# Down units of the expert layer stored with two 128-column blocks interleaved, and x's halves moved in SBUF

## The chip, the cores and the metric

The kernel runs on one core of a Trainium2 chip. The metric is the device time of one execution in microseconds (us). Engines are named as in the profile: PE is TensorE (its weight loads are listed apart, as PEld), DVE is VectorE, ACT is ScalarE, POOL is GpSimd, SP is the engine whose queue issues most DMAs.

## The reference

A transformer block pair in float32 on 256 tokens of width 1024. The part that the change is in is the expert layer (`peer_ffn`): of 16384 experts every token and head picks 16, and the layer needs, for each picked expert e, `gelu(u_e . x)` and then a weighted sum of rows `v_e`:

```python
u = expert_down[eidx]
a = jax.nn.gelu(jnp.einsum('thkd,td->thk', u, xb), approximate=False)
coef = (g * a.astype(jnp.float32)).astype(xb.dtype)
return jnp.einsum('thk,thkd->td', coef, expert_up[eidx])
```

The kernel doesn't gather. It computes `u_e . x` for all 16384 experts and all 256 tokens (the first pass over the experts, with `expert_down`), makes a dense matrix of coefficients that is zero where an expert is not picked, and multiplies it by all of `expert_up` (the second pass).

## The kernel before

**Precision.** Large products are made in fp32r, a float32 format that PE streams at one column a cycle. Each operand is split in a high half (a rounded copy, by ACT) and a low half (the rest, by DVE), and a product is three matmuls: high by high, high by low, low by high.

**Units.** The experts come from HBM in 256 units of 128 partitions x 1024 words (512 KB), units 0 to 127 for the first pass and 128 to 255 for the second. SP loads a unit to `raw_u` (4 buffers), ACT writes `hi_u` (3 buffers, L1586), DVE writes `lo_u` (2 buffers, L2299). A unit of the first pass holds 128 experts; its partition p and block k of 128 words hold element 128k+p of each expert's row, so that block k is the stationary operand of one step over the width.

**The first pass.** `down_unit(u, out)` waits for the unit's halves and runs over k = 0..7. In each step it issues three matmuls with 256 moving columns: stationary `hi_u` block k with moving `xh[:, k, :]` (L938), the same stationary block with moving `xl[:, k, :]` (L941), stationary `lo_u` block k with moving `xh[:, k, :]` (L942). These are 24 matmuls a unit and 3072 in all. Each has its own weight load of 128 columns, 128 consecutive words of each partition. The program prints the operands of a matmul as moving, stationary: `bank<-xh,hi_u` streams `xh` over weights from `hi_u`.

**What DVE does beside it.** In the first two thirds of the pass DVE also picks the experts (steps of `route`, listed at L2196, L2203, L2210, L2213, L2217, L2239 and others). A hand-written table (`ROUTE`) places these steps between the `lo_u` writes of units 0 to 81, in program order. `lo_u` of unit u can be written when the first matmul of unit u-1 has been done (its buffer is then free, `unit_used`), and PE starts unit u when `lo_u` of u is there (`unit_split`). From pair 20 on, PE also runs groups of four 128-column float32 matmuls of one-hot rows (L950, `oh`) between units.

**Addresses.** Tensors are placed by word offset in the partition. All base addresses that matter here are told modulo 128 words, since each block k starts a multiple of 128 words after its tensor's start. `hi_u` and `lo_u` (and `whi`, `wlo`, the same place) start at 80. Before the change `xh` and `xl` both start at 64, which is 16 words below the weights. `xmh` and `xml`, which share the space, start at 96. In the two stages that multiply by the up-projections of the later feed-forward layers (22 slots of 48 matmuls each; they run through 1200 to 1290 us and 1510 to 1590 us) the moving halves `nh`, `nl` both start 16 words below the weights too. `xh` and `xl` are also operands of 456 matmuls of the first projections (L605 to L607, from 11.8 to 78 us), where the weights `whi`, `wlo` are packed.

Of the kernel before, what the change touches and what calls it, by code (L numbers as in the profile page):

```python
# [36 lines left out]
P = 128  # L37
# [3 lines left out]
KD = D // P  # L41
# [10 lines left out]
UNIT = KD * P  # L52
# [145 lines left out]
def program(nc, t):  # L198
    with ExitStack() as ctx:
# [32 lines left out]
        keep = Area(0)  # L232
        h = keep("h", TB, D)

        CROSSING_AT = keep.at
        keep.at += 64
        XH = keep.at
        xh = keep("xh", KD, T, dt=F32R)
        xl = keep("xl", KD, T, dt=F32R)
        keep.at += 64  # L240
        mixed = Area(XH + 32)
        xmh = mixed("xmh", KD, T, dt=F32R)
        xml = mixed("xml", KD, T, dt=F32R)
        cols = keep("cols", N_COLS)
# [310 lines left out]
        def _(pe):  # L555
# [121 lines left out]
            for tb in range(TB):  # L677
                pe.wait_ge(S(f"x_loaded{tb}"), 16)
                for k in range(KD):
                    i, c = k // 2, k % 2  # L680
                    mm = pe.transpose(banks[i][:, c * T + tb * P:c * T + (tb + 1) * P], h[:, tb, k * P:(k + 1) * P], ident)
# [4 lines left out]
            for i in range(4):  # L686

                if i < 3:
                    pe.wait_ge(S("first_low"), i + 1)
                    w = [x.rearrange("p (k n) -> p k n", k=KD) for x in (whi[:, 0, :], wlo[:, 0, :])]  # L690
                else:
                    w = slot("in", 0)
                mm = rows_of(0, i, bank, outs_T(bank), w, xn)
# [4 lines left out]
            for half in range(2):  # L698
                if half == 0:
                    pe.wait_ge(S("second_low"), 1)  # L700
                    w = [x.rearrange("p (k n) -> p k n", k=KD) for x in (whi[:, 1, :], wlo[:, 1, :])]
                else:
                    w = slot("in", 1)
                for c in range(2):
                    for k in range(4 * half, 4 * half + 4):
                        mm = three(bank[:, c * T:(c + 1) * T], [p[:, k, c * P:(c + 1) * P] for p in w], [x[:, k, :] for x in xn],
                                   k == 0 and c == 0, k == KD - 1, True)
            close(mm)
            free_slot()
            w = slot("in", 2)  # L710
# [4 lines left out]
            mm = product_T(bank[:, T:2 * T], w, P, xn)  # L715
# [5 lines left out]
            w = slot("in", 5)  # L721
# [28 lines left out]
            for tb in range(TB):  # L750
                mm = pe.transpose(bank[:, tb * P:(tb + 1) * P], avT[:, tb * P:(tb + 1) * P], ident)
# [3 lines left out]
            for q in range(2):  # L755
                for tb in range(TB):
                    mm = pe.transpose(bank[:, 8 * q + 4 * tb:8 * q + 4 * tb + 4],
                                      gates[0:4, 5 + q, tb * P:(tb + 1) * P], ident[0:4, 0:4])
            close(mm)
            pe.wait_ge(S("const_loaded"), 16)  # L760
            for g in range(2):
                bank = open_("mrow", g)
                for c in range(2):
                    hd = 2 * g + c
                    mm = pe.matmul(bank[:, c * T:(c + 1) * T], cst("sel")[0:4, hd * P:(hd + 1) * P], gates[0:4, 7, :],
                                   start=True, stop=True)
# [7 lines left out]
            for hd in range(4):  # L774
                bank = open_("mscore", hd)
                o = HALF * (hd % 2)
                q, k = qkT[o:o + HALF, hd // 2, :], qkT[o:o + HALF, 2 + hd // 2, :]
# [11 lines left out]
            for hd in range(4):  # L789
                bank = open_("mout", hd)  # L790
                for tb in range(TB):
                    out = bank[:, tb * (P + 1):(tb + 1) * (P + 1)]
                    mm = pe.matmul(out, mE[:, hd, tb * P:(tb + 1) * P], mv[:, 0, hd, :], start=True, stop=(tb == 0))
                    if tb == 1:
                        mm = pe.matmul(out, mE[:, hd, T:T + P], mv[:, 1, hd, :], start=False, stop=True)
# [4 lines left out]
            for hd in range(8):  # L800
                bank = open_("wT", hd)
                pe.transpose(bank[:, 0:P], wS[:, hd * P:(hd + 1) * P], ident)
                for kb in range(2):
                    a = 1024 + hd * T + kb * P
                    mm = pe.transpose(bank[:, P * (1 + kb):P * (2 + kb)], wS[:, a:a + P], ident)
# [5 lines left out]
            for g in range(2):  # L811
                bank = open_("wout", g)
                for c in range(2):
                    for kv in range(2):
                        hd = 4 * kv + 2 * g + c
                        o = HALF * kv
                        out = bank[o:o + HALF, c * T:(c + 1) * T]
                        pe.matmul(out, av[:, 0, o:o + HALF], wT[:, hd, 0:T], start=True, stop=False)
                        mm = pe.matmul(out[:, P:T], av[:, 1, o:o + HALF], wT[:, hd, T:T + P], start=False, stop=True)
# [4 lines left out]
            for tb in range(TB):  # L824
                bank = open_("hmT", tb)
                for c in range(4):
                    mm = pe.transpose(bank[:, c * P:(c + 1) * P], hm[:, tb, c * P:(c + 1) * P], ident)
# [39 lines left out]
            for g in range(2):  # L867
                drained("xq", 2 * g, 2 * g + 1)
                for tb in range(TB):
                    bank = open_("xscore", 2 * g + tb)  # L870
                    for c in range(2):
                        hd = 2 * g + c
                        for dc in range(2):
                            mm = pe.matmul(bank[:, c * T:(c + 1) * T], xqT[:, 2 * hd + dc, tb * P:(tb + 1) * P],
                                           kxT[:, 2 * hd + dc, :], start=(dc == 0), stop=(dc == 1))
# [44 lines left out]
            def unit(u):  # L920

                pe.wait_ge(S("unit_split"), u + 1)
                return hi_u[:, u % HIGH_U, :], low_unit(u)
# [6 lines left out]
                    freeing(ins)  # L930

            def down_unit(u, out):
                w = unit(u)
                for k in range(KD):
                    if u == 0 and k % 2 == 0:
                        pe.wait_ge(S("xn_split"), k // 2 + 1)
                    kp = slice(k * P, (k + 1) * P)
                    mm = pe.matmul(out, w[0][:, kp], xh[:, k, :], start=(k == 0), stop=False)  # L938
                    if k == 0:
                        unit_done(mm, u)  # L940
                    pe.matmul(out, w[0][:, kp], xl[:, k, :], start=False, stop=False)  # L941
                    mm = pe.matmul(out, w[1][:, kp], xh[:, k, :], start=False, stop=(k == KD - 1))  # L942
                return mm

            def spread_group(g):
# [47 lines left out]
            for c in range(P - 2):  # L993
                if c % 2 == 0:
                    pe.wait_ge(S("coef_low"), c // 2 + 1)
                w = unit(P + c)
# [1696 lines left out]
def pack(inp):  # L2693

    g = {k: np.asarray(v) for k, v in inp.items()}
    one = lambda k: g[k].reshape(g[k].shape[1:]) if g[k].shape[0] == 1 else g[k]

    def slots(w):

        out = []  # L2700
        for a in range(0, w.shape[1], 256):
            piece = w[:, a:a + 256]
            piece = np.pad(piece, ((0, 0), (0, 256 - piece.shape[1])))
            out.append(piece.reshape(KD, P, 256).transpose(1, 0, 2).reshape(P, -1))
        return out

    def down(w):

        return [w[i:i + 256].reshape(2, P, D).transpose(1, 0, 2).reshape(P, -1) for i in range(0, w.shape[0], 256)]

    def up(w):

        f = w.shape[1] // 2
        return slots(np.concatenate([np.concatenate([w[:, a:a + P], w[:, f + a:f + a + P]], 1) for a in range(0, f, P)], 1))

    w_in = one("w_in")
    zeros = lambda n: np.zeros((D, n), np.float32)

    order = np.concatenate([np.arange(hd * HALF, (hd + 1) * HALF) for c in range(4) for hd in (c, c + 4)])

    gates = [w_in[:, 1536:1540], zeros(28), w_in[:, 1540:1544], zeros(P - 36)]
    w_in = np.concatenate([w_in[:, 0:512]] + gates + [w_in[:, 2056:2184], w_in[:, 1544:2056][:, order],
                           w_in[:, 2184:2312], zeros(P), w_in[:, 512:1536]], 1)
    w_out = one("w_out")
    w_out = np.concatenate([w_out[0:512], w_out[512:][order]], 0)
    w_odd = g["odd_w_in_2"][0]
    w_xv = slots(one("w_xv"))

    w_even = g["even_w_in_2"][0]
    w_even = np.concatenate([w_even[:, 0:1024], w_even[:, 1536:3584], w_even[:, 1024:1536]], 1)  # L2730
    ws = (slots(w_in) + slots(one("w_xk")) + w_xv[0:1] + slots(w_out) + w_xv[1:2] + slots(one("w_xq")) + w_xv[2:4]
          + slots(one("w_xo")) + slots(one("w_pq")) + slots(w_even) + slots(g["even_w_out_2"][0])
          + up(g["ffn_w_up_2"][0]) + down(g["ffn_w_down_2"][0]) + slots(w_odd[:, :256]) + slots(w_odd[:, 3072:]) + slots(w_odd[:, 256:3072])
          + slots(g["odd_w_out_2"][0]) + up(g["ffn_w_up_2"][1]) + down(g["ffn_w_down_2"][1]))
    assert len(ws) == N_SLOTS
    cols = np.zeros((P, N_COLS), np.float32)

    def put(name, a):
        cols[:a.shape[0], COLS[name][0]:COLS[name][0] + COLS[name][1]] = a

    chan = lambda a: a.reshape(-1, P).T
    for name, a in [("g_mix", g["g_mix"][0]), ("g_cross", g["g_cross"][0]), ("g_mem", g["g_mem"][0]),
                    ("g_ffn", g["g_ffn"][0]), ("mix0", g["mix_norm_g_2"][0]), ("mix1", g["mix_norm_g_2"][1]),
                    ("ffn0", g["ffn_norm_g_2"][0]), ("g_final", g["g_final"]), ("ffn1", g["ffn_norm_g_2"][1]), ("conv_b", g["conv_b"][0]),
                    ("cb0", g["ffn_conv_b_2"][0]), ("cb1", g["ffn_conv_b_2"][1])]:
        put(name, chan(a))
    for name, a in [("conv_w", g["conv_w"][0]), ("cw0", g["ffn_conv_w_2"][0]), ("cw1", g["ffn_conv_w_2"][1])]:
        put(name, a.reshape(a.shape[0], -1, P).transpose(2, 1, 0).reshape(P, -1))
    put("b_i", g["b_igate"].reshape(4, 1))
    put("b_f", g["b_fgate"].reshape(4, 1))  # L2750
    put("sb_q", np.tile(g["sb_q_gain_2"][0], 2)[:, None])
    put("sb_k", np.tile(g["sb_k_gain_2"][0], 2)[:, None])
    rows = np.concatenate([g["g_mhead"][0], g["sinks"][0], g["ret_out_gain_2"][0], g["gla_out_gain_2"][0], g["g_final"]])
    down_units = g["expert_down"][0].reshape(P, P, KD, P).transpose(0, 3, 2, 1).reshape(P, P, UNIT)
    experts = np.concatenate([down_units, g["expert_up"][0].reshape(P, P, UNIT)], 0)
    return {
        "x": g["x"][0], "mem": g["mem"][0], "weights": np.stack(ws), "cols": cols, "rows": rows,
        "const": constants(),
        "keysT": np.stack([g["sub_keys1"][0].T, g["sub_keys2"][0].T], 1),
        "experts": experts,  # L2760
        "walpha": np.concatenate([g["gla_w_alpha_2"][0], g["gla_b_alpha_2"]], 0),
    }
# [20 lines left out]
```

## Time and profile before

| | |
|---|---|
| median of 3 runs | 1668.85 us (1668.18, 1668.85, 1672.76) |
| profiled execution, first to last instruction | 1670.5 us; its page gives no other time |
| PE busy | 1652.9 us (99%), 12006 matmuls |
| DVE busy | 1237.3 us (74%) |
| ACT busy | 935.2 us (56%) |
| POOL busy | 242.8 us (15%) |
| first pass over the experts | 268.9 to 690.9 us |

Matmuls are pipelined: a listed duration (279 ns) overlaps the next matmul, so PE is "busy" 99% whatever its pace. What a matmul costs is the distance from its start to the next one's start, called its cadence below.

### The profile page before, as it was taken

Reading aid. Unit: us, or ns where it says so; the run is one execution under the profiler, and the core shown is the slowest. Engines: PE = TensorE matmul, PEld = TensorE weight load, DVE = VectorE, ACT = ScalarE, POOL = GpSimd, SP = SyncE. Lnnn points to the kernel's source line nnn. Section 1 sums busy time; section 2 is a strip of 40 time slices with the busy share of each in tenths; the row PEclk is TensorE's granted clock in tenths of the full one; section 3 lists DMA queues with packets and bytes.
Section 4 is the critical chain, followed back from the end, with each engine's and each line's share of the span. In section 5 each row is a group of like instructions: output and inputs, shape, how many; then the busy total and the mean of one; then the engine's idle time right before and its main releaser. Section 6 shows DMA issues by size and latency. Waiting matters only on the chain.

```text
span 1670.5 us, 30280 instructions
## 1 busy us (share of the span) xinstructions
PE 1652.9 (99%) x12006; PEld 1542.5 (92%) x12006; DVE 1237.3 (74%) x1896; ACT 935.2 (56%) x1139; POOL 242.8 (15%) x333
## 2 busy tenths in 40 slices
PE   8999999999999999999999999999999999999999
PEld 8999999999999999988888888999999888899987
DVE  6875467999998666667676676887888565769974
ACT  7885565555546555545555454786545357565542
POOL 0000000004667676211010110000000000100000
PEclk9999999999999999999999999999999999999999
DMA  7445344776555555777777776533555544345553
GB/s 304 152 152 180 120 159 157 231 233 213 189 178 191 190 189 191 270 240 238 245 235 239 241 238 222 221 133 139 184 185 195 180 174 152 124 156 203 200 188 115
DMA packets 73804, 323.40 MB, mean 194 GB/s; under 512 B 8663, under 2 KB 9047, under 8 KB 55744
## 3 DMA queue, kind: packets, MB, share of 16 engines
q1 hardware_dynamic: 58736, 285.18, 50.1%
q0 software_dynamic: 5568, 19.38, 3.7%
q10 hardware_dynamic: 9360, 16.92, 2.7%
q8 instruction: 95, 1.56, 0.4%
q14 instruction: 45, 0.37, 0.1%
HBM read 303.62 MB, written 17.83 MB: 192 GB/s over the span
## 4 chain that ended last, share of the span: by engine, by line
PE 83%; DVE 12%; ACT 4%; issue 1%; DMA 0%; SPq 0%; ACTq 0%; DVEq 0%
PE bank L605 14%; PE bank L606 13%; PE bank L607 13%; PE bank L986 7%; PE bank L985 7%; PE bank L987 7%; PE bank L938 5%; PE bank L942 5%; PE bank L941 5%; DVE lo_u L2299 3%; PE bank L950 2%; DVE wlo L1914 2%; DVE oh L2310 1%; ACT whi L1350 1%; DVE pos L2196 1%
## 5 line engine op out<-in xcount | busy, mean ns | idle before, releaser
L1586 ACT ACTIVATE hi_u<-raw_u 128x1024 fp32r<-128x1024 f32 x256 | 271.8, 1062 | 279.6 <-PE bank L985 165.2
L1914 DVE TENSOR_TENSOR wlo<-raw,whi 128x2048 fp32r<-128x2048 f32 (+1 forms) x141 | 314.7, 2232 | 105.6 <-PE bank L605 83.3
L1350 ACT ACTIVATE whi<-raw 128x2048 fp32r<-128x2048 f32 x137 | 263.1, 1920 | 77.6 <-PE bank L605 74.7
L938 PE MATMUL bank<-xh,hi_u 128*128 128x256 f32 x1024 | 291.9, 285 | 1.5 <-DVE lo_u L2299 1.2
L2299 DVE TENSOR_TENSOR lo_u<-raw_u,hi_u 128x1024 fp32r<-128x1024 f32 x192 | 237.9, 1239 | 70.4 <-PE bank L938 62.4
L941 PE MATMUL bank<-xl,hi_u 128*128 128x256 f32 x1024 | 285.4, 279 | 0.0
L942 PE MATMUL bank<-xh,lo_u 128*128 128x256 f32 x1024 | 285.3, 279 | 0.0
L605 PE MATMUL bank<-nh,whi 128*128 128x256 f32 x904 | 253.4, 280 | 0.5 <-DVE wlo L1914 0.4
L607 PE MATMUL bank<-nh,wlo 128*128 128x256 f32 x904 | 251.9, 279 | 0.0
L606 PE MATMUL bank<-nl,whi 128*128 128x256 f32 x904 | 251.9, 279 | 0.0
L519 POOL TENSOR_SCALAR oh<-kept,sel_T 128x128 f32<-128x128 f32 x256 | 199.9, 797 | 249.3 <-ACT sel_T L1636 166.4
L985 PE MATMUL bank<-hi_u,chi 128*128 128x512 f32 x512 | 200.9, 392 | 0.3 <-DVE lo_up L2299 0.3
L987 PE MATMUL bank<-hi_u,clo 128*128 128x512 f32 x512 | 198.7, 388 | 0.0
L938 PEld LDWEIGHTS bank<-xh,hi_u 128*128 128x128 f32 x1024 | 193.0, 188 | 3.4 <-issue 1.5
L941 PEld LDWEIGHTS bank<-xl,hi_u 128*128 128x128 f32 x1024 | 193.4, 189 | 0.0
L942 PEld LDWEIGHTS bank<-xh,lo_u 128*128 128x128 f32 x1024 | 192.8, 188 | 0.0
L607 PEld LDWEIGHTS bank<-nh,wlo 128*128 128x128 f32 x904 | 171.3, 190 | 0.0
L605 PEld LDWEIGHTS bank<-nh,whi 128*128 128x128 f32 x904 | 169.8, 188 | 1.5 <-DVE wlo L1914 1.1
L606 PEld LDWEIGHTS bank<-nl,whi 128*128 128x128 f32 x904 | 170.0, 188 | 0.0
L2299 DVE TENSOR_TENSOR lo_up<-raw_u,hi_u 128x1024 fp32r<-128x1024 f32 x64 | 78.4, 1226 | 96.1 <-PE bank L985 96.1
L985 PEld LDWEIGHTS bank<-hi_u,chi 128*128 128x128 f32 x512 | 96.1, 188 | 23.0 <-DVE lo_up L2299 0.7
L605 PE MATMUL bank<-whi,nh 128*128 128x256 f32 x408 | 115.4, 283 | 0.8 <-DVE nl L1895 0.7
(417 smaller groups left out, 3358.7 us busy)
## 6 DMA issues: line engine op xcount, KB each, us to landing
raw<-in_weights SPq DMA_DIRECT2D x138, 1024.0 KB, 4.8
raw_u<-in_experts SPq DMA_DIRECT2D x256, 512.0 KB, 4.2
aside<-a_out ACTq DMA_DIRECT2D x64, 256.0 KB, 3.6
a_in<-aside POOLq DMA_DIRECT2D x64, 256.0 KB, 3.7
const<-in_const SPq DMA_DIRECT2D x1, 1409.0 KB, 9.0
const<-in_const POOLq DMA_DIRECT2D x1, 1409.0 KB, 6.4
h<-in_x SPq DMA_DIRECT2D x2, 512.0 KB, 5.1
raw<-in_weights SPq DMA_DIRECT2D x2, 512.0 KB, 7.6
```

Source lines behind the costliest of these rows:

```text
L605: freeing(pe.matmul(out, lhs[0], rhs[0], start=first, stop=False, skip_group_check=skip))
L606: pe.matmul(out, lhs[0], rhs[1], start=False, stop=False, skip_group_check=skip)
L607: return pe.matmul(out, lhs[1], rhs[0], start=False, stop=last, skip_group_check=skip)
L938: mm = pe.matmul(out, w[0][:, kp], xh[:, k, :], start=(k == 0), stop=False)
L941: pe.matmul(out, w[0][:, kp], xl[:, k, :], start=False, stop=False)
L942: mm = pe.matmul(out, w[1][:, kp], xh[:, k, :], start=False, stop=(k == KD - 1))
L985: first = pe.matmul(out, c_hi, w[0][:, cs], start=(c == 0), stop=False)
L987: mm = pe.matmul(out, c_lo, w[0][:, cs], start=False, stop=(c == P - 1))
L1350: a(A(whi[:, n % HIGH, :], raw[:, n % RAW, :], ACT.Copy), S("weights_hi"))
L1586: a(A(hi_u[:, u % HIGH_U, :], raw_u[:, u % RAW_U, :], ACT.Copy), S("unit_high"))
L1914: v(V.tensor_tensor(wlo[:, n % LOW, place], raw[:, n % RAW, place], whi[:, n % HIGH, place].bitcast(F32), ALU.subtract), S("weights_split" ...
L2299: v(V.tensor_tensor(low_unit(u), raw_u[:, u % RAW_U, :], hi_u[:, u % HIGH_U, :].bitcast(F32), ALU.subtract), S("unit_split"))
```

## The change

The host stores the blocks of a down unit in pairs, with the words of blocks 2j and 2j+1 alternating; the elementwise splits by ACT and DVE and the DMAs run over the same 1024 words as before. A weight load of block k now reads every second word of 256 consecutive ones, starting at word k % 2. Besides, `xh` moves to 16 (modulo 128 words, 64 below the weights, counted round) and `xl` to 112 (32 above them). The total space and the places of `xmh`, `xml`, `chi`, `clo` and everything else stay. No engine's instructions change in number or order, and no wait is added or removed.

```diff
         CROSSING_AT = keep.at
-        keep.at += 64
+        keep.at += 16
         XH = keep.at
         xh = keep("xh", KD, T, dt=F32R)
+        keep.at += 96
         xl = keep("xl", KD, T, dt=F32R)
-        keep.at += 64
-        mixed = Area(XH + 32)
+        keep.at += 16
+        mixed = Area(CROSSING_AT + 96)
...
             def down_unit(u, out):
-                w = unit(u)
+                w = [x.rearrange("p (k n c) -> p k c n", c=2, n=P) for x in unit(u)]
...
-                    kp = slice(k * P, (k + 1) * P)
-                    mm = pe.matmul(out, w[0][:, kp], xh[:, k, :], start=(k == 0), stop=False)
+                    mm = pe.matmul(out, w[0][:, k // 2, k % 2, :], xh[:, k, :], start=(k == 0), stop=False)
                     if k == 0:
                         unit_done(mm, u)
-                    pe.matmul(out, w[0][:, kp], xl[:, k, :], start=False, stop=False)
-                    mm = pe.matmul(out, w[1][:, kp], xh[:, k, :], start=False, stop=(k == KD - 1))
+                    pe.matmul(out, w[0][:, k // 2, k % 2, :], xl[:, k, :], start=False, stop=False)
+                    mm = pe.matmul(out, w[1][:, k // 2, k % 2, :], xh[:, k, :], start=False, stop=(k == KD - 1))
...
-    down_units = g["expert_down"][0].reshape(P, P, KD, P).transpose(0, 3, 2, 1).reshape(P, P, UNIT)
+    down_units = g["expert_down"][0].reshape(P, P, KD // 2, 2, P).transpose(0, 4, 2, 1, 3).reshape(P, P, UNIT)
```

## Rows read from the trace of the kernel before

**Rows 1.** The page: span, and busy time, share and instructions of each engine.
```profile
span 1670.5 us, 30280 instructions
PE 1652.9 (99%) x12006; PEld 1542.5 (92%) x12006; DVE 1237.3 (74%) x1896; ACT 935.2 (56%) x1139; POOL 242.8 (15%) x333
```

**Rows 2.** Stretches of the first pass: busy (instructions) of PE, PEld, DVE, ACT, POOL; clock.
```profile
268.89:525.03 256.14, 254.69 (x2181) 252.70 (x2180) 243.11 (x610) 139.33 (x163) 92.79 (x118) 1.00 0.63 205
525.03:690.88 165.85, 165.85 (x1445) 165.85 (x1444) 104.93 (x198) 90.14 (x114) 109.32 (x143) 1.00 0.58 198
```

**Rows 3.** The same stretches, L950's one-hot matmuls alone.
```profile
268.89:525.03 256.14, 29.47 (x224) 1.00 0.63 205
525.03:690.88 165.85, 37.95 (x288) 1.00 0.58 198
```

**Rows 4.** Timeline of PE: first matmuls of units 16 and 17, 24 matmuls apart.
```profile
318.08 0.28 PE L938 MATMUL bank<-xh,hi_u 128*128 128x256 f32 x1
...
320.90 0.28 PE L938 MATMUL bank<-xh,hi_u 128*128 128x256 f32 x1
```

**Rows 5.** Timeline of PE: first matmuls of units 33 and 34, 24 matmuls apart.
```profile
366.39 0.28 PE L938 MATMUL bank<-xh,hi_u 128*128 128x256 f32 x1
...
369.12 0.28 PE L938 MATMUL bank<-xh,hi_u 128*128 128x256 f32 x1
```

**Rows 6.** Timeline of PE: runs of plain float32 matmuls, start and length of each run.
```profile
168.53 7.07 PE L874 MATMUL bank<-kxT,xqT 128*128 128x256 f32 x32
1362.62 1.03 PE L592 MATMUL bank<-kept,h 128*128 128x128 f32 x8
271.72 3.73 PE L907 MATMUL bank<-keysT,pqT 128*128 128x128 f32 x32
```

**Rows 7.** Timeline of PE: the second pass, 512 moving columns.
```profile
800.02 0.39 PE L985 MATMUL bank<-hi_u,chi 128*128 128x512 f32 x1
800.25 0.39 PE L986 MATMUL bank<-lo_up,chi 128*128 128x512 f32 x1
800.48 0.39 PE L987 MATMUL bank<-hi_u,clo 128*128 128x512 f32 x1
800.71 0.39 PE L985 MATMUL bank<-hi_u,chi 128*128 128x512 f32 x1
```

**Rows 8.** Stretches of two later stages, PE alone: busy (matmuls), clock.
```profile
1200.00:1290.00 90.00, 90.00 (x767) 1.00 0.53 188
1510.00:1590.00 80.00, 80.00 (x709) 1.00 0.55 195
```

**Rows 9.** Waits of DVE from 268 to 525 us: total, times, longest.
```profile
DVE lo_u L2299 <- PE bank L938: 4.0, 6, 2.1
```

**Rows 10.** Waits of DVE from 525 to 691 us.
```profile
DVE lo_u L2299 <- PE bank L938: 58.4, 45, 2.5
```

**Rows 11.** Timeline of DVE in the first stretch, with no wait in it.
```profile
434.23 1.29 DVE L2213 TENSOR_TENSOR onehot<-posf,kept 128x1024 f32<-128x1024 f32 x1
435.55 1.28 DVE L2299 TENSOR_TENSOR lo_u<-raw_u,hi_u 128x1024 fp32r<-128x1024 f32 x1
436.87 1.27 DVE L2217 TENSOR_TENSOR onehot<-onehot,i16f 128x1024 f32<-128x1024 f32 x1
438.17 1.28 DVE L2299 TENSOR_TENSOR lo_u<-raw_u,hi_u 128x1024 fp32r<-128x1024 f32 x1
```

**Rows 12.** Timeline of DVE in the second stretch; in brackets the idle time ahead.
```profile
603.13 1.28 DVE L2299 TENSOR_TENSOR lo_u<-raw_u,hi_u 128x1024 fp32r<-128x1024 f32 x1 [1.24 <-PE bank L938]
604.45 1.17 DVE L2310 TENSOR_SCALAR oh<-kept,sel_T 128x128 f32<-128x128 f32 x4
606.76 1.28 DVE L2299 TENSOR_TENSOR lo_u<-raw_u,hi_u 128x1024 fp32r<-128x1024 f32 x1 [1.14 <-PE bank L938]
```

**Rows 13.** Matmuls with `xh` outside the first pass: count, durations, first and last start.
```profile
L605 PE MATMUL bank<-xh,whi x88: 276/281/582, 11.8 to 44.6; 128*128 128x256 f32 x88
L605 PE MATMUL bank<-whi,xh x64: 276/279/388, 49.0 to 77.5; 128*128 128x256 f32 x64
```

## The prediction

> **What bounds the kernel now.** I read the page first: PE is busy 1652.9 of 1670.5 us [rows 1]. That number says only that PE's queue is rarely empty, because listed durations overlap. So I read the starts. In the first pass the timeline shows two paces for the same instructions. Unit 16 takes 320.90 - 318.08 = 2.82 us for 24 matmuls, 117.7 ns each [rows 4]. Unit 33 takes 2.73 us, 113.6 ns each [rows 5]. The granted clock is 1.00 in both, the 2.4 GHz level, at which 256 columns take 106.7 ns; so 7 ns or 11 ns a matmul are lost. The same pair of paces stands in two later stages that run the same form of matmul: 90.00 us over 767 records, less the about three that began earlier, is 117.8 ns, and 80.00 over 706 is 113.3 ns [rows 8]. Both numbers are multiples of one step over 106.7: three matmuls take 320 ns of streaming, and 340 or 353.3 ns here, which is 3 or 5 steps of 6.67 ns (16 cycles). In the second pass three matmuls of 512 columns take 800.71 - 800.02 = 0.69 us against 0.64 of streaming, about 7 steps [rows 7].
>
> Plain float32 runs lose less. 32 matmuls of 256 columns take (7.07 - 0.38)/31 = 216 ns, two cycles a column being 213.3. Eight transposes take (1.03 - 0.27)/7 = 109 ns for 128 columns (106.7 of streaming), and the key products (3.73 - 0.27)/31 = 111.6 ns [rows 6]. What differs is the reading speed. In those runs a column of the moving operand takes two cycles. In fp32r it takes one, while the weights of the next matmul, 128 words, must come in during about the same 113 ns. So the stream walks through SBUF at about twice the pace of the load beside it, and the distance between the two changes by 128 words in each matmul. In the plain runs of 128 columns both walk 128 words in the same time.
>
> Next, who sets the time of the pass. It has two parts. From 268.89 to 525.03 us (units 0 to 79) DVE is busy 243.1 of 256.1 us and waits for PE only 4.0 us [rows 2, 9]; its timeline is back to back, `lo_u` between steps of the routing [rows 11]. There DVE sets the time, or nearly. From 525.03 to 690.88 us (units 80 to 127) DVE waits for PE 58.4 us, over a microsecond ahead of each `lo_u` [rows 10, 12], and PE sets the time.
>
> **The change, part by part.** The instructions of all engines, their order and waits stay, and so do the bytes and shapes of the DMAs and splits; these cost 0. What changes is only how PE's two readings run.
>
> *The load with a step of two words.* It now walks 256 words while the stream walks 256. If the lost steps come from the two meeting in SBUF at equal addresses modulo some period, a distance that stays constant (64 or 32 words, never 0) has no meeting. The trace of before shows no load with a step, so I bound the new cadence. Below: 109 ns, the transposes. Above, if the load reads twice the stretch and pays twice, 2 x 106.7 = 213 ns. Between them the marks are 111.6 (key products), 113.3, 117.8 and one step more on each matmul, 124.4. I take 110: the plain runs, whose two readings walk together, are the rows that the new pattern is nearest to.
>
> The Trainium skill has a rule that bears on this (SBUF — State Buffer, Door 1: The DMA port swizzle, the note on cachelines): full read speed needs at least two hits in each 16-byte line. A step of two float32 words gives exactly two hits, so by the rule the load pays nothing; no row here shows a step.
>
> *The second stretch.* It holds 48 x 24 = 1152 of the matmuls and 288 of L950 [rows 3]. With 111.6 ns for each of these (as the key products, the same form), the cadence is (165.85 - 288 x 0.1116)/1152 = 116.1 ns. At 110 it saves 1152 x 6.1 = 7.0 us. DVE has a spare microsecond a unit, so nothing takes its place.
>
> *The first stretch.* PE at 110 would need 1920 x 0.110 + 224 x 0.1116 + 3.7 for the key products = 239.9 us, less than DVE's 243.1 plus its gaps. So DVE alone sets the time, and the gain is what DVE waits for PE now, 4.0 us. The longest of the six waits, 2.1 us, stands at unit 2, behind the key products, and is hardly touched by the cadence. I count 4.0 - 2.1 = 1.9 us. This is the cover that hides most of the edit: without it 1920 x 6 ns = 11.5 us would come.
>
> *xh and xl at other distances, weights packed.* (88 + 64) x 3 = 456 matmuls of the first projections [rows 13]. They can fall to either pace: 456 x 4.4 ns = 2.0 us each way. I take 0.
>
> Sum: -7.0 - 1.9 = -8.9 us, so 1670.5 becomes 1661.6 in the profile's execution, and the median 1668.85 becomes 1660.
>
> *Luck in later stages.* Which of the two paces a stage falls into isn't fixed by its addresses: the two stages of [rows 8] stand at the same distance, 16 words, and run differently. Each has 22 x 48 = 1056 such matmuls, so one that changes pace moves the time by 4.7 us. The three runs of before, 1668.2, 1668.9 and 1672.8, lie just so far apart. The change shifts every later start and may flip one either way. It is in the range and not in the sum.
>
> **The rivals.**
> - *One pace, 113.3* (15%). The smaller loss belongs to fp32r itself, and the interleaving removes only the larger. For it: none of the fp32r rows here is below 113. Second stretch 1152 x 2.8 = 3.2 us, first about 1: 1664.7.
> - *Nothing happens* (15%). The load and the stream don't disturb each other, and the two paces come from somewhere else, such as how the queue feeds PE. Against it: the loss grows from 3 or 5 steps to 7 with 512 columns [rows 7], which a cost per instruction wouldn't; yet the load is no longer there, and a meeting of load and stream should not grow either. This is the weak place of my mechanism. 1668.9. The Trainium skill says as much (TensorE: Matmul & The Clock Gate, Step-by-step: what each phase is for): the operands have separate read ports, and loading weights takes nothing from a running matmul. By that rule the sum is 0; the two paces of one instruction speak against its being the whole story.
> - *The new pattern locks at 117.8* (13%). Second stretch 1152 x 1.7 = 2.0 us; in the first PE needs 1920 x 0.1178 + 25.0 + 3.7 = 254.9 us of 256.1, and it can't make up the moments in which it waits for DVE: about 2 more. 1672.8.
> - *Slower: the load pays for the step* (17%). With a step of two, a load touches twice the stretch of SBUF: it has twice the chance to meet the stream, or simply runs slower. It decides as soon as the mean is above about 118 ns. One step more, 124.4: first stretch 1920 x 0.1244 + 28.7 = 267.5 us, +11.4; second 1152 x 8.3 = 9.6: 1690. In the extreme the load doubles to 213 ns and adds 3072 x 97 ns = 298 us: 1967. I give the extreme 4 of the 17.
>
> **How the numbers follow.** The forecast (cadence 109 to 112, 1655 to 1663 by itself with a flip of a later stage) has 40%, the rivals 15, 15, 13 and 17. The measurement tells about 0.3%, 5 us, from no change. Faster: nearly all of the forecast (37), and where the first rival meets a lucky flip (6): 43%. Slower: 17 of the last rival, 5 of the fourth, 2 of bad luck: 24%. Same: 33%. The range leaves out the last rival and little of the tails: the low end is the forecast with a flip, 1655, less one for the first projections; the high end is 1672.8 with a flip, 1677.5: 1654 to 1678.
>
> **What would show it.** The starts of L938 to L942 in the profile of the changed kernel. Right: 24 matmuls in 2.62 to 2.68 us in units after 80, DVE's waits ahead of `lo_u` there down by about 7 us in total, the first stretch shorter by about 2 us only, with PE now waiting for `lo_u` at many unit starts. The second pass keeps its 0.69 us for three. Wrong: 2.72 or 2.83 us units as before (second to fourth rival), or units of 2.95 us and more with DVE's waits grown in both stretches (the last). If the gain of the first stretch exceeded 4.0 us, my reading that DVE sets its time would be wrong. If the second stretch gained as forecast and the time did not, a later stage has changed its pace, and its starts would show it.

## The result and the profile after

The changed kernel takes 1677.31 us (median of 6 runs, 1676.21 to 1682.71) against 1668.57 us of the kernel before beside it (6 runs): ratio 1.0051, 95% interval [1.0038, 1.0065]. It is slower by about half a per cent. I had forecast 1660, a gain of 9 us; the loss is 8.7 us.

The page of the changed kernel, span and engines, answers to [rows 1]:

```profile
span 1675.7 us, 30280 instructions
PE 1659.7 (99%) x12006; PEld 1551.0 (93%) x12006; DVE 1237.5 (74%) x1896; ACT 935.3 (56%) x1139; POOL 248.5 (15%) x333
```

The two stretches of the first pass (units 0 to 79, units 80 to 127), columns as in [rows 2]:

```profile
269.44:529.32 259.88, 259.88 (x2181) 259.59 (x2180) 243.88 (x612) 139.38 (x164) 99.11 (x119) 1.00 0.61 202
529.32:700.05 170.73, 170.73 (x1446) 170.73 (x1444) 104.18 (x196) 89.97 (x113) 108.69 (x142) 1.00 0.57 192
```

The timeline of PE, two first matmuls of a step, 24 matmuls apart, in the first stretch; before they were 2.82 or 2.73 us apart [rows 4, 5]:

```profile
318.02 0.28 PE L938 MATMUL bank<-xh,hi_u 128*128 128x256 f32 x1
...
320.90 0.28 PE L938 MATMUL bank<-xh,hi_u 128*128 128x256 f32 x1
```

Waits of DVE in the first stretch, then in the second, answer to [rows 9, 10]:

```profile
DVE lo_u L2299 <- PE bank L938: 6.8, 12, 2.1
...
DVE lo_u L2299 <- PE bank L938: 63.5, 46, 2.5
```

The number to look at is 320.90 - 318.02 = 2.88 us, 120.0 ns a matmul. Of the 127 distances between the starts of neighbouring units 39 are 2.880 us to the nanosecond, none is shorter than 2.879, and the two paces of before are gone. The second stretch is 4.9 us longer (170.73 against 165.85), the first 3.7 us. In the first, PE was busy 254.7 of 256.1 us before [rows 2]; now it has no idle time at all (259.88 of 259.88), and DVE, which waited 4.0 us for it, waits 6.8. The two engines had been about level there, and now PE alone sets the time. The whole first pass costs 8.6 us more, and the first projections, where `xh` and `xl` have moved and the weights are packed, 0.5 (the pass begins at 269.4 instead of 268.9 us). That last number is small beside the scatter of the pass's start from profile to profile: a second profile of before, `before_again` below, has 269.1, and the other runs below have 269.0 to 271.9.

The profiled spans differ by 5.2 us only, because in the first profile of before a later stage ran at its slow pace. A window on the first stage of the up-projections in the changed kernel, and below it, from `before_again`, the window that [rows 8] has:

```profile
1210.00:1300.00 90.00, 90.00 (x797) 1.00 0.57 199
```

```profile
1200.00:1290.00 90.00, 90.00 (x796) 1.00 0.57 199
```

In [rows 8] this stage held 767 matmuls in 90 us, 117.8 ns each; here both kernels hold 796 or 797, 113.4 ns. Every run's time is its span and 1.8 us, so the first profile of before (1670.5) stands for a run of about 1672.3, where four of the six runs beside the changed kernel took 1668.0 to 1668.9. The medians differ by 8.7 us, about the 8.6 of the pass and the 0.5 of the first projections.

### The profile page after: what moved, and what is told of

Read it like the earlier page. It is cut to its first block, busy times and chain, and to the rows that moved or that the text cites. A ratio compares the mean times of both kernels' runs of the same rounds, so it can differ in the third digit from the quotient of the medians.

```text
span 1675.7 us, 30280 instructions
## 1 busy us (share of the span) xinstructions
PE 1659.7 (99%) x12006; PEld 1551.0 (93%) x12006; DVE 1237.5 (74%) x1896; ACT 935.3 (56%) x1139; POOL 248.5 (15%) x333
## 4 chain that ended last, share of the span: by engine, by line
PE 91%; DVE 4%; ACT 4%; issue 1%; DMA 0%; SPq 0%; DVEq 0%; ACTq 0%
PE bank L606 13%; PE bank L607 13%; PE bank L608 13%; PE bank L941 7%; PE bank L942 7%; PE bank L938 7%; PE bank L987 7%; PE bank L986 7%; PE bank L985 7%; PE bank L950 3%; DVE wlo L1914 2%; ACT whi L1350 1%; ACT wS L1472 1%; PE bank L593 0%; PE bank L908 0%
## 5 line engine op out<-in xcount | busy, mean ns | idle before, releaser
L941 PE MATMUL bank<-xl,hi_u 128*128 128x256 f32 x1024 | 290.6, 284 | 0.0
L942 PE MATMUL bank<-xh,lo_u 128*128 128x256 f32 x1024 | 290.0, 283 | 0.0
L520 POOL TENSOR_SCALAR oh<-kept,sel_T 128x128 f32<-128x128 f32 x256 | 205.6, 820 | 251.4 <-ACT sel_T L1636 168.9
L942 PEld LDWEIGHTS bank<-xh,lo_u 128*128 128x128 f32 x1024 | 201.6, 197 | 0.0
L941 PEld LDWEIGHTS bank<-xl,hi_u 128*128 128x128 f32 x1024 | 201.5, 197 | 0.0
L938 PEld LDWEIGHTS bank<-xh,hi_u 128*128 128x128 f32 x1024 | 200.1, 195 | 0.3
```

Of the source, the lines that this page charges most:

```text
L938: mm = pe.matmul(out, w[0][:, k // 2, k % 2, :], xh[:, k, :], start=(k == 0), stop=False)
L941: pe.matmul(out, w[0][:, k // 2, k % 2, :], xl[:, k, :], start=False, stop=False)
L942: mm = pe.matmul(out, w[1][:, k // 2, k % 2, :], xh[:, k, :], start=False, stop=(k == KD - 1))
```

## The experiments

**Each half of the change alone.** `step_only` is the changed kernel with

```diff
-        keep.at += 16
+        keep.at += 64
         XH = keep.at
         xh = keep("xh", KD, T, dt=F32R)
-        keep.at += 96
         xl = keep("xl", KD, T, dt=F32R)
-        keep.at += 16
-        mixed = Area(CROSSING_AT + 96)
+        keep.at += 64
+        mixed = Area(XH + 32)
```

> The interleaved units and the step of two words as in the change, but xh and xl left where they were, 16 words below the weights. Theory A (the step itself costs): every matmul of the first pass has the cadence of the changed kernel, 120.0 ns (2.88 us for a unit of 24), at any distance; first pass about 430 us long against 422 before, and about 1677 us in all. Theory B (the step is fine, the new distances of 64 and 32 words are bad): a constant distance of 16 words gives 113.3 ns or less, units of 2.72 us or shorter, and 1665 us or less.

`places_only` is the kernel before with the opposite edit: packed units, `xh` and `xl` 64 below and 32 above the weights.

> Units packed as before, only xh and xl moved to 64 below and 32 above the weights. Theory A (the step costs): the first pass keeps its two paces, units of 2.72 or 2.83 us, and the time is that of before, 1668.6 us, give or take the 4.7 us of a later stage's flip. Theory B (the distances cost): units of about 2.88 us here too, and 1675 us or more. In the first projections the changed kernel already showed cadences of 119 to 124 ns that before didn't have, so both theories expect those here, some 1 us.

Stretches of the first pass, PE alone, in `step_only`:

```profile
271.13:531.10 259.97, 259.97 (x2182) 1.00 0.61 202
531.10:701.94 170.84, 170.84 (x1445) 1.00 0.56 192
```

and in `places_only`:

```profile
271.85:529.43 257.58, 257.09 (x2181) 1.00 0.62 204
529.43:697.83 168.40, 168.40 (x1445) 1.00 0.57 195
```

`step_only`: 1677.23 us, ratio 1.0034 [1.0021, 1.0047]; its pass is that of the full change within 0.2 us. `places_only`: 1674.87 us, ratio 1.0024 [1.0008, 1.0039]; its pass takes 426.0 us against 422.0. Both ratios are to 19 runs of before on the same chip, which had a median of 1672.1 us there instead of 1668.6 and spread from 1667 to 1675; so the passes are the better comparison. Theory A holds for the step: it alone makes the whole loss of the pass, wherever the halves lie. What it expected of the places failed, since they are not neutral for packed units. None of the units of `places_only` takes less than 2.80 us, so the fast pace of before is gone there too, and with the sum of the prediction the second stretch gives (168.40 - 288 x 0.1116)/1152 = 118.3 ns. The two halves don't add up, since the step sets 120 ns over either.

**The matmuls by themselves.** Four runs hold nothing but sections of 48 to 96 matmuls, each section on its own line of the program, so that the timeline merges it to one row: its start, its length, its line and the count. The cadence is (length - 0.28)/(count - 1), with 0.28 us for the listed duration of the last matmul (0.40 where the load has a step of four). The first matmuls of a section are slower; "in steady state" below is the mean distance of the last 25 starts. A plain float32 matmul of the program stands in the trace as two records, and each counts as one here.

```python
for u, k, i in three(4):
    a, first, last = out(u, i, k, 256)
    pe.matmul(a, stepped(2)(sel(wf, i), k), X(48 if i != 1 else 48, i == 1, k, 256), start=first, stop=last)
```

> Leaves out the whole model. It is a chain of sections of 96 matmuls in fp32r with 256 moving columns in the order of the first pass (high by xh, high by xl, low by xh), with nothing running beside them, in which only the distance between moving and stationary operand (0 to 112 words in steps of 16, and the pair 64 and 32) and the step of the weight load (1, 2, 4, 8 words) change; each twice, behind 4 and behind 7 plain float32 matmuls. Theory A: step 1 gives 113.3 or 117.8 ns at every distance, by luck of the start; step 2 gives 120 ns at every distance, step 4 and 8 more. Theory B: step 2 has distances with about 109 to 113 ns and others at 120 or more, and the pair 64 and 32 is one of the bad ones. A third one, that the cadences come from what the other engines do to SBUF meanwhile: here, with all of them idle, everything is at 109 ns.

The sweep's rows: packed at 0, 16, 32 and 48 words (L88 to L100); a step of two at 0 and 48 (L124, L136); a step of four at 0 (L232):

```profile
31.60 11.76 PE L88 MATMUL bank<-x,wf 128*128 128x256 f32 x96
44.01 11.55 PE L92 MATMUL bank<-x,wf 128*128 128x256 f32 x96
56.20 11.64 PE L96 MATMUL bank<-x,wf 128*128 128x256 f32 x96
68.49 11.15 PE L100 MATMUL bank<-x,wf 128*128 128x256 f32 x96
...
141.18 11.77 PE L124 MATMUL bank<-x,wf 128*128 128x256 f32 x96
...
178.43 11.78 PE L136 MATMUL bank<-x,wf 128*128 128x256 f32 x96
...
486.59 22.65 PE L232 MATMUL bank<-x,wf 128*128 128x256 f32 x96
```

With all other engines idle the cadences are those of the kernel, so neither ACT, DVE nor the DMAs have a part in them. Packed: 11.48/95 = 120.8, 118.6, 119.6 and 114.4 ns over the whole section; in steady state 120.0, 117.8, 118.7 and 113.3. The distance matters, and each distance gives what the one 64 words farther gives. With the step of two it doesn't matter: all eight distances and the pair of the change, behind both starts, settle at 120.0. The idea on which I built the forecast, a constant distance without meetings, is refuted by this alone. So at 0 words, where the packed load is at 120.0 already, the step costs nothing, and at 48 words it costs 6.7 ns. With a step of four the cadence is (22.65 - 0.40)/95 = 234.2 ns over the section, 233.3 to 235.6 in steady state; with a step of eight it is 240 to 241. The price is therefore not in proportion to the stretch that the load walks over: two costs some ns, four doubles the cadence, and eight adds hardly anything to that.

> Leaves out the whole model: sections that change the stream's length (128 to 512 columns), the load (packed, step of two words, 64 or 32 columns wide, all 128 columns from one word) and the format (fp32r or plain float32), at distances of 48 and 0 words. Theory A (the load with a step reads twice as much of SBUF and meets the stream more often): at 256 columns step two is at 120, packed at 113.3 for 48; with 64 or 32 columns of load, or all from one word, the loss over 106.7 shrinks to some 3 ns; at 128 columns the load sets the cadence, and the step of two shows its own duration, above 107 ns. Rival (the loss is the stream's own, the load has no part): narrow loads keep 113 to 120 ns at 256 columns. In plain float32 the stream reads at half the pace: theory A expects 109 to 112 ns for both steps, or a little more for the step of two.

Sections of `load_law`: fp32r with 128 columns of stream, packed (L93) and step of two (L97), at 48 words; plain float32 with 128 columns, step one (L253) and two (L257); plain float32 with 256 columns, step one (L261) and two (L265); and fp32r with 512 columns at 0 words, packed (L197) and step of two (L201):

```profile
33.38 5.55 PE L93 MATMUL bank<-x,wf 128*128 128x128 f32 x48
39.63 5.86 PE L97 MATMUL bank<-x,wf 128*128 128x128 f32 x48
...
246.60 11.17 PE L197 MATMUL bank<-x,wf 128*128 128x512 f32 x48
258.42 11.44 PE L201 MATMUL bank<-x,wf 128*128 128x512 f32 x48
...
381.39 10.88 PE L253 MATMUL bank<-f 128*128 128x128 f32 x96
393.00 11.47 PE L257 MATMUL bank<-f 128*128 128x128 f32 x96
405.20 20.89 PE L261 MATMUL bank<-f 128*128 128x256 f32 x96
426.81 20.89 PE L265 MATMUL bank<-f 128*128 128x256 f32 x96
```

> Leaves out the whole model: sections as in the sweeps, with the load 32, 64 or 96 columns wide, packed and with a step of two words, at 256 columns of stream; and with the full load at 208 to 288 columns of stream, both steps. Theory A (the step makes the load longer, 117.8 ns against 111.7 for 128 columns, and it shows where load and stream are equally long): a load of 32 or 64 columns with the step is done early and costs no more than a packed one, within 1 ns; with the full load the step costs 6 ns up to 240 columns of stream and less than 2 ns from 272 on. Rival (each line read by the load disturbs the stream, whatever the load's length): the narrow loads with the step cost more than the packed ones, in proportion, at every width, and 288 columns pay as well.

Sections of `narrow_steps` at 48 words, packed and step of two by turns: load 64 columns wide (L104, L108); full load at 240, 256, 272 and 288 columns of stream (L184 to L212); and at 0 words, 64 wide (L128, L132); L360 is L192 once more behind another start:

```profile
57.26 11.66 PE L104 MATMUL bank<-x,wf 128*64 128x256 f32 x96
69.57 11.35 PE L108 MATMUL bank<-x,wf 128*64 128x256 f32 x96
129.92 11.14 PE L128 MATMUL bank<-x,wf 128*64 128x256 f32 x96
141.71 11.76 PE L132 MATMUL bank<-x,wf 128*64 128x256 f32 x96
287.69 8.31 PE L184 MATMUL bank<-x,wf 128*128 128x240 f32 x72
296.64 8.73 PE L188 MATMUL bank<-x,wf 128*128 128x240 f32 x72
306.02 8.42 PE L192 MATMUL bank<-x,wf 128*128 128x256 f32 x72
315.10 8.89 PE L196 MATMUL bank<-x,wf 128*128 128x256 f32 x72
324.63 9.14 PE L200 MATMUL bank<-x,wf 128*128 128x272 f32 x72
334.42 9.45 PE L204 MATMUL bank<-x,wf 128*128 128x272 f32 x72
344.51 9.85 PE L208 MATMUL bank<-x,wf 128*128 128x288 f32 x72
355.00 9.85 PE L212 MATMUL bank<-x,wf 128*128 128x288 f32 x72
...
769.01 8.73 PE L360 MATMUL bank<-x,wf 128*128 128x256 f32 x72
```

The step costs (8.73 - 8.31)/71 = 5.9 ns at 240 columns, 6.6 at 256, 4.4 at 272 and 0 at 288. Up to 240 columns that is what theory A says. At 272 it had said less than 2 ns, since the packed cadence there, 123.3 in steady state, is longer than a load of 117.8; behind the other start the step cost 3.3, and at 28 words 1.1 and 0. A half-wide load at 48 words pays nothing for the step (in steady state 119.0 ns packed, 115.6 with the step). At 0 words it does, 113.3 against 120.0 (117.8 behind the other start), which theory A doesn't give either. So there is a second effect, of the step and the places together, as large as the first one, and both theories missed it. L192 and L360 are the same section: 113.3 and 117.8 ns in steady state.

**The change made stronger, and halved.** `step4` interleaves four blocks, `every_other` only the even units; both leave `xh` and `xl` where they were. The edit of `every_other` to the kernel before begins so; the indices and the host's storing of the units follow it:

```diff
-                w = unit(u)
+                c = 2 - u % 2
+                w = [x.rearrange("p (k n c) -> p k c n", c=c, n=P) for x in unit(u)]
...
```

> The change made stronger: four blocks interleaved, the load of the first pass reads every fourth word; xh and xl at the old places. Theory A (the load pays for the stretch that it reads, and nothing but the 107 ns of the stream hides it): 233.3 ns a matmul as in the sweep, a first pass of 3072 x 0.2333 + 512 x 0.1116 + 3.7 = 778 us against 422, and about 2025 us in all; the load, not DVE, sets both stretches. If something else in the kernel made the changed units slow (DVE, the DMAs, the order of the stored data), the time would stay near 1677 us.

> Half of the change: the even units interleaved and read with a step of two words, the odd ones packed; xh and xl at the old places. Theory A: 120 ns in the even units and 113.3 or 117.8 in the odd ones, so 2.88 us and 2.72 to 2.83 us by turns behind unit 80, about half of the loss of step_only: 1671 to 1674 us. Rival (interleaving makes the whole pass fall in another steady state, whichever units have it): all or no units at 2.88 us.

Two starts of `step4` three matmuls apart (timeline of PE), then what its DVE waits for through the pass:

```profile
1042.05 0.40 PE L937 MATMUL bank<-xh,hi_u 128*128 128x256 f32 x1
...
1042.76 0.40 PE L937 MATMUL bank<-xh,hi_u 128*128 128x256 f32 x1
...
DVE lo_u L2298 <- PE bank L937: 429.0, 127, 5.3
```

Its one run took 2031.9 us (expected 2025): the cadence is (1042.76 - 1042.05)/3 = 0.237 us, double. The page of the same run has DVE at 1234.2 us of work (1237.3 before). `every_other`: 1671.10 us, ratio 1.0014 [1.0001, 1.0027], beside 13 runs of before at 1669.0. First matmuls of unit 125 (packed), of unit 126 (interleaved) and of unit 127:

```profile
686.94 0.28 PE L938 MATMUL bank<-xh,hi_u 128*128 128x256 f32 x1
...
689.67 0.28 PE L938 MATMUL bank<-xh,hi_u 128*128 128x256 f32 x1
...
692.55 0.28 PE L938 MATMUL bank<-xh,hi_u 128*128 128x256 f32 x1
```

2.73 us packed, 2.88 interleaved: each unit has the cadence of its own loads. Half of the units cost rather a third than half of the loss: from unit 0 to its end the pass takes 424.8 us, 2.8 more than in the first profile of before, where `step_only` takes 8.8 more.

**Is there a better place?**

> Leaves out the whole model: sections of 72 packed fp32r matmuls as in the first sweep, at distances of 0 to 60 words in steps of 4, each behind 4, 5, 6 and 7 plain float32 matmuls. The first sweep gave 120, 117.8, 118.7 or 120, and 113.3 ns at 0, 16, 32 and 48 words, the same at 64 words more. Theory C (the distance modulo 64 words sets the cadence of packed loads): one value for each distance whatever comes ahead, 113.3 around 48 words, 120 around 0. Theory D (several steady states, and the start picks one): some distances show 113.3 behind one number of matmuls and 117.8 behind another, as the kernel before did at 48 modulo 64. A distance below 113 ns anywhere would mean that the floor of fp32r is lower than the kernel ever had.

Sections of the fine sweep at 28 words (L121, L185; L249 and L313 show the same) and at 16 words (L109, L173):

```profile
71.45 8.73 PE L109 MATMUL bank<-x,wf 128*128 128x256 f32 x72
99.76 8.45 PE L121 MATMUL bank<-x,wf 128*128 128x256 f32 x72
222.64 8.41 PE L173 MATMUL bank<-x,wf 128*128 128x256 f32 x72
251.43 8.46 PE L185 MATMUL bank<-x,wf 128*128 128x256 f32 x72
```

Both theories have part of it (all numbers in steady state): twelve of the sixteen distances have one value within 0.3 ns, but 16 words shows 117.8 (L109) or 113.3 (L173) by the start, and 20, 32 and 36 words have two values as well. 28 and 48 words settle at 113.3 in all four; none is below. For 48 words `load_law` and `narrow_steps` each have a section in the second state, 117.8.

> Units packed as before; xh and xl 28 words above the weights (modulo 128) instead of 16 below. The fine sweep had 113.33 ns at 28 words behind every one of four starts. Theory E (28 words has one steady state): every unit behind unit 80 takes 2.72 us without groups, the first pass 417 to 419 us against 421.9, and the time is 3 to 4 us below before. Rival (the kernel finds a second state here too, as it did at 16 below, where the sweep also saw only 113.33): units of both 2.72 and 2.83 us and no difference.

> As at28_pass, and the halves of the later stages moved as well: those that stream over packed weights 28 words above them, those that are the stationary side 28 below the streaming weights (nh, nl, xmh, xml). Theory E: the stages of the up-projections run at 113.33 ns in every execution, so the time lies 6 to 12 us below before and the runs scatter less than the 4.7 us of a flip. Rival: these stages still take either pace, and nothing is gained beyond at28_pass.

> The kernel before, unchanged, profiled once more. If the stages after the first pass fall into either pace by luck of the start, this profile has another set of paces than the first one (the stage of the up-projections from 1200 us at 113.3 ns instead of 117.8, for instance), and its span differs by the sum of them, in steps of about 4.7 us for each of the two large stages. If the paces are set by the addresses, it has the same set and the same span within 1 us.

Stretches of `at28_pass`, PE alone, then the first matmuls of units 125 and 127, 48 matmuls apart:

```profile
270.32:525.84 255.52, 254.06 (x2182) 1.00 0.64 205
525.84:691.15 165.31, 165.31 (x1446) 1.00 0.59 198
...
682.99 0.28 PE L949 MATMUL bank<-xh,hi_u 128*128 128x256 f32 x1
...
688.43 0.28 PE L949 MATMUL bank<-xh,hi_u 128*128 128x256 f32 x1
```

`at28_pass` shows one state only, as expected: units of 2.72 us, (688.43 - 682.99)/2. But it gains little: 1667.28 us, ratio 0.9996 [0.9987, 1.0005], no difference that can be told from the 1668.2 of before beside it, and the pass takes 420.8 us where I expected 417 to 419. Behind every group of L950 a unit needs a few matmuls to settle at this distance, 115.5 ns in the mean over the first twenty in the sweep. `at28_all` was a miss: 1674.39 us, ratio 1.0038 [1.0025, 1.0052]. Where the weights are the stream over `nh` or `xmh`, 28 words gave close to 120 ns, while the two stages of the up-projections ran at 113.3 in its profile as they do in `before_again`, so that nothing could be won there. PE's records in the same 20 us of a stage of the first kind, `at28_all` first and `before_again` below:

```profile
1066.00:1086.00 20.00, 20.00 (x171) 1.00 0.44 159
```

```profile
1066.00:1086.00 20.00, 19.93 (x176) 1.00 0.45 167
```

The order in which operands repeat is another there than in my sweeps, so their values can't be carried over. `before_again` took 1667.61 us and its span is 1665.8 us, 4.7 below the first profile. It showed another set of paces with the same program and addresses: 796 matmuls in the window above instead of 767, while the second stage of [rows 8] is at its fast pace in both. So the addresses don't fix the pace. In the fine sweep the number of matmuls ahead chooses it at some distances; what chooses it in the kernel stays open.

## Why the prediction was wrong

- **The bound of each stretch.** The second is PE's, as read. In the first I had DVE alone, and that was too simple: 1920 x 0.1177 + 28.7 = 254.7 us is what PE needs there at its slow pace, and it was busy 254.7 of 256.1 us; I had the same sum in the rival "locks at 117.8". The two were level, so a slower PE had no cover at all. The cover on the other side is real: `at28_pass` has faster units, and its first stretch is shorter by 0.6 us only. The sums hold for the cadence that came. With 120.0 instead of 110 the second stretch is (170.73 - 32.1)/1152 = 120.3 ns, 1152 x 4.2 = 4.8 us more, measured 4.9. For the first, 1920 x 0.120 + 28.7 = 259.1 us, measured 259.9.
- **The step that failed** is "I take 110: the plain runs, whose two readings walk together, are the rows that the new pattern is nearest to." The plain runs said nothing of walking together. They show 111.6 at 128 columns and 215.8 at 256 because there either the load alone is seen or the stream hides it, at 0 words as well as at 48. The key products' 111.6 in [rows 6] was the price of a packed load of 128 columns and a lower bound of the cadence, in sight and not read as such. With the step this price rises to 117.8, and at 256 columns of fp32r stream the cadence is 120.0 instead of 110.
- **How much of the loss the load's price explains.** The second stretch went from 116.1 to 120.3 ns a matmul. A load of 117.8 makes the first 1.7 ns of that unavoidable, 2.0 us of the 4.9. That the cadence is 120.0 and not 117.8 makes the other 2.9 us. The runs show it at every distance and have no reason for it; 120.0 is also what packed loads of 111.7 ns settle at with 0 words between.
- **"A distance that stays constant has no meeting"** fell with it: no distance does better than 120 with the step. That meetings exist at all is borne out only in part: for packed loads the distance decides between 113.3 and 120, but the floor of 113.3 stands with a load of 32 columns as well. The weak place that I named, the loss with 512 columns, was a real one: no section with 512 columns is below 226.7 ns, 13.3 above the streaming, at any distance and width of load.
- **The rival that came true** is "the load pays for the step", to which I gave 17%, at 120.0 ns instead of the 124.4 that I priced, so 8.6 us instead of 21. Its mechanism was half right. The load does run slower with the step. Whether it also disturbs the stream more is not settled: the loads of half the width say yes at 0 words and no at 48. By its own price the load would give the 117.8 of the rival "locks at 117.8". The units of 2.88 us fit none of the signs that I had named, 2.72, 2.83 or 2.95 and more. By the Trainium skill's rule (SBUF — State Buffer, Door 1: The DMA port swizzle, the note on cachelines), the step of two words should be at full speed. The trace agrees in the large, since the doubling comes with the step of four, where a line gives one hit, and a step of eight, with one hit too, adds hardly anything (234 and 241 ns). But 6 ns of 112 are paid at two hits.
- **Luck in later stages** was right for one of the two stages. The first stage took 125.5 us in the first profile of before and 121.3 in `before_again`, 4.2 us apart where I had said 4.7, and in the profile of `step_only` it was slow again; the second took 121.3 us in every profile. The run of 1672.76 fits that, but has no second profile to show it. I had set the sum from the profile with the slow stage against a median without it.
- **The range** of 1654 to 1678 contains the 1677.3 by luck. Its top was made of a pass at 117.8 and a later stage that turns slow. The pass was worse than that, and in the changed kernel's profile the later stage was not slow.
- **What was forecast of the first projections**, 2.0 us either way and 0 taken, came to about 0.5 us of loss, less than the start of the pass moves between profiles.

## What to carry to other kernels

A weight load has a price of its own, and it shows as soon as the stream is not longer: read it from a run of matmuls with a short stream before changing how weights are stored. At 256 columns of fp32r a packed load (111.7 ns) just fits beside the stream (113.3 at best), and one with a step of two words (117.8) doesn't. In plain float32 at 256 columns the step was free. In fp32r with longer streams don't count on that: it was free at 288 and 320 columns, and cost up to 6.7 ns at 512, by the places of the operands. When two profiles of a kernel differ, compare the starts of equal stages first: a pace that the addresses don't fix was worth 4.2 us here, half of what the change did.

## What the runs showed of the hardware

At a granted clock of 1.00 (2.4 GHz) a load of 128 packed columns takes 111.7 ns, with a step of two words 117.8; with a step of four the cadence at 256 columns is 233 to 236 ns, with eight 240 to 241. In fp32r 256 columns never took less than 113.3 ns, whatever the distance and the width of the load. Packed at 256 columns the steady cadence depends on the distance of the two operands modulo 64 words, from 113.3 (28 and 48 words) to 120.0 (0 words); the cadences of the kernel's first pass (113.3 and 117.8 at 16 words below, 117.8 for `places_only`, 120.0 with the step) came back with the rest of the core idle. At 16, 20, 32, 36 and 48 words there are two steady states, and the start chooses. What makes these states, why a load of 117.8 and a stream of 113.3 make 120.0 together, and why the step costs something at 384 and 512 columns in some places, is open.
